# A hybrid decoder trunk with top-2 experts: token lists of all experts from one set of products, expert loops of two engines written out, one projection part moved

## The reference, cut to what matters

```python
D_MODEL, SEQ, N_EXPERTS, TOP_K, D_FF_EXPERT = 1024, 256, 8, 2, 1792

def swiglu(h, w_gu, w_down, d_ff):
    gu = h @ w_gu
    return (jax.nn.silu(gu[..., :d_ff]) * gu[..., d_ff:]) @ w_down

def moe_ffn(h, w_router, w_gu, w_down):
    B, S, D = h.shape
    ht = h.reshape(B * S, D)
    logits = (ht @ w_router).astype(jnp.float32)
    top_vals, top_idx = lax.top_k(logits, TOP_K)
    top_w = jax.nn.softmax(top_vals, axis=-1)
    combine = jnp.sum(jax.nn.one_hot(top_idx, N_EXPERTS, dtype=jnp.float32) * top_w[..., None], axis=1)
    out = jnp.zeros((B * S, D), jnp.float32)
    for e in range(N_EXPERTS):
        y = swiglu(ht, w_gu[e], w_down[e], D_FF_EXPERT)
        out = out + combine[:, e:e + 1] * y.astype(jnp.float32)
    return out.astype(h.dtype).reshape(B, S, D)

# per layer
x = x + token_mixing(rms_norm(x, norm_mix_g[i]), ...)
x = x + swiglu(...) if i % 2 == 0 else x + moe_ffn(rms_norm(x, norm_ffn_g[i]), ...)
h = rms_norm(x, norm_ple_g[i])
x = x + sigmoid(h @ ple_w_gate[i]) * (p[i] @ ple_w_proj[i])
```

## Time and profile before

| | |
|---|---|
| median of 3 runs | 1281.6 us |
| the profiled execution | 1283.54 us |
| its span (first to last instruction) | 1281.8 us |
| TensorE busy | 1216.9 us, 95% |
| VectorE busy | 905.9 us, 71% |
| ScalarE busy | 741.2 us, 58% |
| GpSimd busy | 115.2 us, 9% |
| mean granted TensorE clock | 0.986 |
| chain that ended last, TensorE's share | 78% |

### The profile page before, as it was taken

The page is one execution under the profiler, slowest core; times in us unless marked ns, Lnnn a source line. Parts: engine busy times, 40 slices in busy tenths (PEclk is TensorE's granted clock), DMA queues, the critical chain, the costliest instruction groups (busy, mean ns, idle before and its releaser), DMA issues.

```text
span 1281.8 us, 16174 instructions
## 1 busy us (share of the span) xinstructions
PE 1216.9 (95%) x5978; PEld 1011.5 (79%) x5978; DVE 905.9 (71%) x892; ACT 741.2 (58%) x700; POOL 115.2 (9%) x130
## 2 busy tenths in 40 slices
PE   5999999999999998999999699999999999999977
PEld 4997788788888876997788587777777878787855
DVE  5667756645545566667855678888898888888975
ACT  4536543543543455437443477777777777777753
POOL 3520000200000010420000100000000000001210
PEclk9999999999999999999999899999999999999988
DMA  9845455655555554645454579999999999999941
GB/s 306 289 147 189 140 180 182 191 179 190 196 191 175 191 180 148 195 158 173 135 180 162 179 281 361 373 363 372 367 371 369 370 370 371 358 382 369 391 164 49
DMA packets 167153, 318.47 MB, mean 248 GB/s; under 512 B 6640, under 2 KB 70384, under 8 KB 167104
## 3 DMA queue, kind: packets, MB, share of 16 engines
q1 hardware_dynamic: 161792, 302.01, 67.8%
q0 software_dynamic: 4192, 13.95, 3.0%
q10 hardware_dynamic: 1120, 1.85, 0.4%
HBM read 312.03 MB, written 5.77 MB: 248 GB/s over the span
## 4 chain that ended last, share of the span: by engine, by line
PE 78%; DVE 8%; ACT 7%; issue 4%; DMA 1%; POOL 1%; ACTq 0%; DVEq 0%; SPq 0%; POOLq 0%
PE ps L1591 19%; PE ps L1578 11%; PE ps L1505 10%; PE ps L1357 9%; PE ps L1359 9%; PE ps L1358 9%; PE ps L1519 6%; ACT split L593 5%; DVE split L875 4%; PE ps L1373 1%; DMA raw<-w_in_dram 1%; PE ps L1559 1%; PE ps L1427 1%; DVE M L1162 1%; ACT L593 1%
## 5 line engine op out<-in xcount | busy, mean ns | idle before, releaser
L875 DVE TENSOR_TENSOR split<-raw,split 128x2048 fp32r<-128x2048 f32 x286 | 655.0, 2294 | 258.7 <-ACT split L593 257.8
L593 ACT ACTIVATE split<-raw 128x2048 fp32r<-128x2048 f32 x286 | 546.3, 1915 | 242.3 <-PE ps L1359 103.8
L1591 PE MATMUL ps<-split,br 128*128 128x512 f32 x1344 | 322.7, 395 | 6.9 <-DVE split L875 5.3
L1591 PEld LDWEIGHTS ps<-split,br 128*128 128x128 f32 x1344 | 250.8, 189 | 62.5 <-DVE split L875 9.0
L1357 PE MATMUL ps<-split,hT 128*128 128x512 f32 (+1 forms) x416 | 166.0, 399 | 9.6 <-DVE split L875 4.0
L1578 PE MATMUL ps<-split,hT 128*128 128x512 f32 x672 | 159.1, 392 | 8.7 <-DVE hT L1045 8.7
L1358 PE MATMUL ps<-split,hT 128*128 128x512 f32 (+1 forms) x416 | 161.2, 388 | 0.0
L1359 PE MATMUL ps<-split,hT 128*128 128x512 f32 (+1 forms) x416 | 161.2, 388 | 0.0
L1578 PEld LDWEIGHTS ps<-split,hT 128*128 128x128 f32 x672 | 124.9, 188 | 37.2 <-DVE split L875 11.8
L1505 PE MATMUL ps<-split,hT 128*128 128x512 f32 x576 | 136.5, 392 | 0.5 <-DVE tmp L991 0.5
L1505 PEld LDWEIGHTS ps<-split,hT 128*128 128x128 f32 x576 | 107.1, 188 | 23.3 <-DVE tmp L991 1.2
(11 more groups left out here) (225 smaller groups left out, 1037.6 us busy)
## 6 DMA issues: line engine op xcount, KB each, us to landing
raw<-moe_w_gu_dram SPq DMA_DIRECT2D x96, 1024.0 KB
raw<-moe_w_down_dram SPq DMA_DIRECT2D x56, 1024.0 KB
raw<-w_in_dram SPq DMA_DIRECT2D x46, 1024.0 KB
raw<-ffn_w_gu_dram SPq DMA_DIRECT2D x56, 512.0 KB
raw<-moe_w_gu_dram SPq DMA_DIRECT2D x32, 512.0 KB
raw<-ffn_w_down_dram SPq DMA_DIRECT2D x14, 1024.0 KB
raw<-w_branch_dram SPq DMA_DIRECT2D x12, 1024.0 KB
raw<-w_out_dram SPq DMA_DIRECT2D x8, 1024.0 KB
```

The costliest lines, as they stand in the source:

```text
L593: act.activation(split[:, t % SPLIT, 0, :], raw[:, t % RAW, :], ACT.Copy).then_inc(hi, 1)
L875: dve.tensor_tensor(split[:, t % SPLIT, 1, :], raw[:, t % RAW, :], split[:, t % SPLIT, 0, :].bitcast(F32), ALU.subtract).then_inc(lo, 1)
L1591: ins = pe.matmul(ps[:, 5 if kind == "up" else 4, :], xe[:, sl, 4 * part + k, :], slot(t, sr, 512)[:, k, :], start=part + k + m == 0, stop ...
```

## The change

1. *Lists.* Each token has two picks (k = 0, 1), each with a place in its expert's list (`place2`, from the product with the triangle, masked by `hot`). `build_lists` makes one one-hot matrix for each of 2 token blocks and 2 picks (into `prT`), `tok_hot` holds the token number under its expert's column, and `lists` sums four products to a 128 x 8 matrix: the lists of all eight experts at once. `route`, `take_slots` and the one-hots inside the loop go; G is built for the last expert only.
2. *Loops.* The first pass of the experts is written out in Python on ScalarE and VectorE (TensorE and SyncE keep their loops; the second pass keeps all).
3. *Order in an expert.* The eviction of the transposed activation (tiles 5, 11, 17) is put ahead of that tile's split, on both engines.
4. *Weights.* The weights, rows and picks go into expert 1, at tiles 6, 9 and 12.
5. *Before the experts.* The two token blocks' logits go to banks of their own and VectorE takes them one after the other. The transposes of block 1 come ahead of `proj_part(0, 1)`, `proj_part(1, 0)` behind the second logits, `proj_part(1, 1)` behind the rank; its eviction goes behind the exponential and a split on ScalarE. The tokens-per-expert count has its own product and signal.

```diff
+AT_WEIGHTS = (6, 9, 12)
...
-            def rows_of(s, i, j):
+            def rows_of(s, i):
-                pool.wait_ge(slots_ready[s], j + i)
-                pool.indirect_dma_start(rows_in, None, y_rows[:, :], bass.IndirectOffsetOnAxis(slot_tok[:, 0:1], 0)
+                pool.indirect_dma_start(rows_in, None, y_rows[:, :],
+                                        bass.IndirectOffsetOnAxis(slot_tok[:, i:i + 1], 0)
...
@@ ScalarE, expert @@
+                    if j in AT_EVICT:
+                        act.wait_ge(a_turned[s], AT_EVICT.index(j) + 1 + i * (LAST_F + 1))
+                        act.activation(aT_moe[:, 0], ps[:, 6, :].rearrange("p (k n) -> p k n", k=4), ACT.Copy
+                                       ).then_inc(aT_hi[s], 1)
                     if not last or j + 2 < BODY_TILES:
                         split_hi(t0 + j + 2, i, BODY_TILES, s)
...
-                    if j in AT_EVICT:
-                        act.wait_ge(a_turned[s], AT_EVICT.index(j) + 1 + i * (LAST_F + 1))
-                        act.activation(aT_moe[:, 0], ps[:, 6, :].rearrange("p (k n) -> p k n", k=4), ACT.Copy
-                                       ).then_inc(aT_hi[s], 1)
...
@@ ScalarE, experts @@
-                with act.Fori(0, EXPERTS - 1) as e:
-                    expert(s, t0, e, False)
+                if s == 1:
+                    for e in range(EXPERTS - 1):
+                        expert(s, t0, e, False)
+                else:
+                    with act.Fori(0, EXPERTS - 1) as e:
+                        expert(s, t0, e, False)
...
                     proj_out_of(1, 0)
-                    proj_out_of(1, 1)
-                    act.wait_ge(sel_ready, 2)
+                    act.wait_ge(sel_ready, 3)
                     act.activation(wts[:, :, 1:2], wts[:, :, 0:1], ACT.Exp).then_inc(route_step, 1)
                     split_hi(t0 + T_OUT + 6)
+                    proj_out_of(1, 1)
                     experts(1, t0 + T_FFN[1])
...
@@ VectorE @@
+            def build_lists(s):
+                for b in range(NB):
+                    for k in range(2):
+                        ins = dve.tensor_scalar(prT[:, 2 * b + k, :], slot_row[:, :], place2[:, s - 1, b, k:k + 1],
+                                                None, ALU.is_equal)
+                ins.then_inc(lists_ready[s], 1)
+                dve.wait_ge(route_done[s], 1)
+                dve.tensor_copy(slot_tok[:, :], ps[:, 7, SEQ:SEQ + EXPERTS]).then_inc(slots_ready[s], 1)
...
-                    if j == 1 and not (last and s == 2):
-                        dve.wait_ge(route_done[s], 1 + i)
-                        if not last:
-                            build_g(s, i + 1 + (EXPERTS if s == 2 else 0), g_ready[s])
+                    if last and s == 1 and j == 1:
+                        build_g()
...
-                    if j == AT_MUL[0] and not last:
-                        dve.wait_ge(rows_landed[s], 16 + i * 16)
-                        take_slots(s, 2 + i)
+                    if j in AT_EVICT:
+                        dve.wait_ge(aT_hi[s], AT_EVICT.index(j) + 1 + i * (LAST_F + 1))
+                        dve.tensor_tensor(aT_moe[:, 1], ps[:, 6, :].rearrange("p (k n) -> p k n", k=4),
+                                          aT_moe[:, 0].bitcast(F32), ALU.subtract).then_inc(aT_lo[s], 1)
                     if not last or j + 2 < BODY_TILES:
                         split_lo(t0 + j + 2, i, BODY_TILES, s)
...
+                    if s == 1 and i == 1 and j == AT_WEIGHTS[0]:
+                        token_weights()
+                    if s == 1 and i == 1 and j == AT_WEIGHTS[1]:
+                        token_rows()
+                    if s == 1 and i == 1 and j == AT_WEIGHTS[2]:
+                        token_picks()
...
+                    for b in range(NB):
+                        dve.wait_ge(logit_done, b + 1)
+                        both = ps[:, LOGIT_BANKS[b], 0:2 * EXPERTS]
+                        chain(dve.tensor_copy(logit[:, b, :], both[:, EXPERTS:]))
+                        chain(dve.tensor_tensor(logit[:, b, :], both[:, 0:EXPERTS], logit[:, b, :], ALU.add))
+                        chain(dve.max(top[:, b, :], logit[:, b, :]))
+                        chain(dve.max_index(topi[:, b, :], top[:, b, :], logit[:, b, :]))
+                        chain(dve.tensor_copy(topf[:, b, :], topi[:, b, :]))
+                        chain(dve.tensor_tensor(
+                            hot[:, b], slot_row[:, 0:EXPERTS].unsqueeze(1).broadcast_to([P, 2, EXPERTS]),
+                            topf[:, b, 0:2].unsqueeze(2).broadcast_to([P, 2, EXPERTS]), ALU.is_equal))
+                        dve.tensor_tensor(sel[:, b, :], hot[:, b, 0, :], hot[:, b, 1, :], ALU.add
+                                          ).then_inc(sel_ready, 1)
...
@@ TensorE @@
-            def route(s, n):
-                pe.wait_ge(g_ready[s], n)
-                pe.wait_ge(tok_ready, NB)
+            def lists(s):
+                pe.wait_ge(lists_ready[s], 1)
                 for b in range(NB):
-                    ins = pe.matmul(ps[:, 7, SEQ:SEQ + 1], G[:, b, :].bitcast(F32), tok_f[:, b:b + 1],
-                                    start=b == 0, stop=b == NB - 1)
+                    for k in range(2):
+                        ins = pe.matmul(ps[:, 7, SEQ:SEQ + EXPERTS], prT[:, 2 * b + k, :], tok_hot[:, b, k, :],
+                                        start=b + k == 0, stop=b + k == NB)
                 ins.then_inc(route_done[s], 1)
...
-                    if j == AT_ROUTE and not last:
-                        route(s, 2 + i)
...
                     logits(0)
+                    turn(6, Y, y_of(4), (2, 3))
                     proj_part(0, 1)
-                    turn(6, Y, y_of(4), (2, 3))
+                    logits(1)
                     proj_part(1, 0)
-                    logits(1)
-                    proj_part(1, 1)
...
-                    pe.matmul(ps[:, 6, 80:88], ones[:, :], sel[:, 0, :], start=True, stop=False)
-                    pe.matmul(ps[:, 6, 80:88], ones[:, :], sel[:, 1, :], start=False, stop=True
+                    pe.matmul(ps[:, 6, 72:80], ones[:, :], sel[:, 0, :], start=False, stop=True
                               ).then_inc(rank_done, 1)
+                    pe.matmul(ps[:, 4, 64:72], ones[:, :], sel[:, 0, :], start=True, stop=False)
+                    pe.matmul(ps[:, 4, 64:72], ones[:, :], sel[:, 1, :], start=False, stop=True
+                              ).then_inc(load_done, 1)
+                    proj_part(1, 1)
+                    lists(1)
```

More of the change, by code:

```diff
@@ L185, in trunk @@
         sel = sb("sel", [P, NB, EXPERTS])
[L186 removed]
+        rank = sb("rank", [P, NB])
         load = sb("load", [P, EXPERTS])
@@ L1067, in experts @@
                     gather_lo(s, half, 0)
-                with dve.Fori(0, EXPERTS - 1) as e:
-                    expert(s, t0, e, False)
+                if s == 1:
+                    for e in range(EXPERTS - 1):
+                        expert(s, t0, e, False)
+                else:
+                    with dve.Fori(0, EXPERTS - 1) as e:
+                        expert(s, t0, e, False)
                 expert(s, t0, EXPERTS - 1, True)
@@ L1272, in _ @@
-                    chain(dve.tensor_scalar(rank[:, :, EXPERTS:2 * EXPERTS], rank[:, :, 0:EXPERTS],
-                                            -float(P), None, ALU.add))
-                    take_slots(1, 1)
-                    chain(dve.tensor_copy(load[:, :], ps[:, 6, 80:88]))
-                    chain(dve.tensor_reduce(most[:, 0:1], load[:, :], AX.X, ALU.max))
+                    earlier = ps[:, 6, 64:80].rearrange("p (b e) -> p b e", b=NB)
+                    for b in range(NB):
+                        ins = dve.tensor_tensor(nth[:, b], hot[:, b],
+                                                earlier[:, b].unsqueeze(1).broadcast_to([P, 2, EXPERTS]), ALU.mult)
@@ L1277, in _ @@
+                    chain(dve.tensor_reduce(most[:, 0:1], ps[:, 4, 64:72], AX.X, ALU.max))
                     chain(dve.tensor_scalar(most[:, 1:2], most[:, 0:1], float(P), None, ALU.is_gt))
@@ L1293, in _ @@
-                    place, first, second, row = (pick[:, i] for i in range(4))
-                    for b in range(NB):
-                        for k in range(2):
-                            ins = dve.tensor_tensor(nth[:, b, k, :], hot[:, b, k, :], rank[:, b, 0:EXPERTS],
-                                                    ALU.mult)
-                    chain(ins)
-                    chain(dve.tensor_reduce(place, nth[:, :, :, :], AX.X, ALU.add))
-                    chain(dve.scalar_tensor_tensor(out=row, in0=topf[:, :, 0:2], scalar=float(P), in1=place,
-                                                   op0=ALU.mult, op1=ALU.add))
@@ L1302, in _ @@
-                    chain(dve.tensor_scalar(second, place, float(P), None, ALU.is_ge))
-                    chain(dve.tensor_scalar(first, second, -1.0, 1.0, ALU.mult, ALU.add))
```

(11 more changed lines are left out.)

119 lines of the change are left out of this document (59 added, 60 removed).

## The result

| | before | after |
|---|---|---|
| runs of the comparison | 7 | 7 |
| median (lowest to highest), us | 1281.78 (1280.89 to 1283.37) | 1265.92 (1265.53 to 1273.95) |
| ratio, 95% interval | | 0.990 [0.9881, 0.9919] |
| profiled execution, us | 1283.5 | 1265.92 |
| span, us; mean granted clock | 1281.8; 0.986 | 1264.2; 0.987 |

The median fell by 15.9 us, 16.1 were forecast. The runs of after come in two groups that have to be kept apart: four at 1265.5 to 1265.9 us, clock 0.986 to 0.987, and three at 1273.5 to 1274.0, clock 0.980; the profiled one belongs to the first. The median lies in the lower group by one run. The ratio takes in both groups: the means are 1269.1 and 1282.0 us, 12.8 us apart.

A forecast was written before the change was run, and what follows sets the result against it. TensorE was taken to bound the kernel, but for holes repeating with every expert. The terms 5.8 + 7.8 + 2.0 - 3.2 + 3.5 - 0.6 + 0.8 = 16.1 us gave 1281.6 - 16.1 = 1265.5 us, range 1261.5 to 1274.

The forecast's parts named there:

- Item 1: ScalarE's loop written out: the table load before an expert's tile 2 goes, 6 x 0.97 = 5.8 us; bounds 0 to 5.8.
- Item 2: Eviction ahead of the split: the hole before tile 18 shrinks, 7.8 us, and 2.0 us more in the last expert.
- Item 3: A new 0.45 us wait before tile 20, on the half-size subtraction, 7 times: -3.2 us; bounds 0 to 4.
- Item 4: No list product or one-hot in the loop: 0.50 x 7 = 3.5 us of TensorE; lower bound 2.5.
- Item 5: Weights and picks at tiles 6, 9 and 12 of expert 1 delay VectorE: -0.6 us; bounds 0 and -4.0.
- Item 6: The start, before the experts: 0.8 us sooner; bounds 1.8 sooner, 1.5 later.
- Its 9.4 us: The most gain the forecast's own terms could lose, used for the slow side of the range.
- the start late: Unfavourable bound for the stretch before the experts: 1.5 us later instead of 0.8 sooner.
- DMA rival: Across the experts, transfers become the limit: 1274 us at 375 GB/s, 1279 at 369; chance 0.10.
- starved ring: Evictions three times an expert delay splits TensorE needs; slower if each comes 1.0 us later than worked out; chance 0.04.

The follow-up runs named there:

- e2_loops: Kernel before, with only the loops of ScalarE and VectorE over experts 0 to 6 written out: 1275.80 us, ratio 0.9949.
- e3_loop_dve: Kernel before, with only VectorE's expert loop written out: 1282.67 us, ratio 1.0002.
- e6_tail: Kernel after, with the half-size eviction and subtraction ahead of the second half of the next expert's gathered rows: 1263.51 us, ratio 0.9864.
- e4_lists: Kernel after, with loops, eviction order and place of weights and picks as before; new lists and order before the experts stay: 1285.10 us, ratio 1.0012.
- e8_all: e7_busy with the order of e6_tail and a Silu of one value right behind the exponential: 1261.92 us, ratio 0.9847.
- e9_full: e10_hole with the order of e6_tail, the early one-value Silu and 20 unread matmuls behind the lists: 1257.93 us, ratio 0.9819.
- e7_busy: e5_part_back with 20 matmuls whose result nothing reads, issued behind the lists for the row gather's wait: 1266.71 us, ratio 0.9880.
- e5_part_back: Kernel after, with projection part (0,1) back ahead of block 1's transposes and (1,0) ahead of the second logits: 1266.43 us, ratio 0.9886.
- e10_hole: Kernel after, with 9 matmuls whose result nothing reads ahead of block 1's transposes: 1265.41 us, ratio 0.9881.
- e1_order: Kernel before, with only the evictions of the transposed activation moved ahead of the split on both engines: 1275.10 us, ratio 0.9941.

## Why the prediction was right, item by item

*Item 1, the table load, 5.8 us.* Right in cause and size. e2_loops gives 5.7 us, e3_loop_dve nothing.

*Item 2, eviction ahead of the split, 7.8 + 2.0 us.* Right. The hole before tile 18 shrank by 1.10 us, as worked out, and the last expert by 2.28.

*Item 3, the wait before tile 20, -3.2 us.* Place, cause and length are right (seven times, 0.42 us, on the half-size subtraction). Its price is not: by starts an expert loses 0.69 us there, not 0.45, since a wait of 0.42 also costs TensorE the overlap of one tile with the next (a tile ahead of a wait lasts 2.99 us; in a run of tiles one starts every 2.72). e6_tail gets 0.60 an expert back. That makes 4.8 us, over the item's bound of 4. The 0.24 us an expert that this is more than forecast don't show in the sum, since they came back elsewhere: 0.13 at the start of the expert, whose tiles 0 to 4 with the first transposes take 13.96 us against 15.56 before, where 1.47 were counted, and the rest in amounts too small to place.

*Item 4, the list product, 3.5 us.* 0.5 us an expert (e4_lists: 62.02 against 62.53), but not in expert 0. There it turned into a wait: with the product gone TensorE reached the first transposes before VectorE had the gated product, which stood behind the Silu table load that the written-out code keeps.
```profile
744.04 1.28 ACT L688 ACT_TABLE_LOAD   x1
```
```profile
733.63 16.54 PE L1612 MATMUL ps<-split,br 128*128 128x512 f32 x60 [0.56 <-DVE br L995]
750.72 0.66 PE L1580 MATMUL ps<-ident,tmp 128*128 128x128 f32 x4 [0.55 <-DVE tmp L1040]
```
Expert 0 was to gain 1.1 + 0.5 - 0.45 = 1.15 us and gained 0.08. Its second part, behind the first transposes, gained 0.49 (46.87 against 47.36); its first part lost 0.41 (17.09 against 16.68), of which the wait is a part; some 0.3 more go to the clock, which stays at half for 5.6 us of expert 0 (733.63 to about 739.2) where it did for 4.9 before (735.93 to about 740.8). The forecast used expert 2 for all seven; half clock and the first load make expert 0 another case. With the early Silu in e8_all and e9_full that wait is gone. No run has the early Silu alone, but the other parts leave the wait as it is: it is 0.55 us in e6_tail, which has the order, and 0.55 in e7_busy, where the clock is full.

*Item 5, weights and picks in expert 1, -0.6 us.* Right in size, not in place: expert 1 is 61.20 us, 0.77 over its neighbours. The prediction lets the first two groups of instructions fit and the third pile up. By starts, 0.52 us go behind the first group, which VectorE begins at 818.82 (TensorE's tiles from 819.84 to 828.52 take 8.68 us, 8.16 in expert 2), and 0.28 behind the third, begun at 836.15 (837.17 to 845.61, 8.44 against 8.16). The instructions moved were 24 before, not 23; nothing hangs on it.

*Item 6, the start, 0.8 us sooner.* The working was right and its frame too small. From the second logits' product to the first expert it is 14.59 us (719.04 to 733.63) against 15.45 before (720.48 to 735.93): 0.86 sooner. But the second logits came 1.20 later behind the first, so the start is 0.34 later. The failed step is that the item followed only the part (1,1). The others move too; the one that goes from ahead of the transposes to behind them leaves TensorE idle 2.89 us instead of 1.40, and the clock falls. The prediction reads the clock in two stretches of an expert, where it is full, and says nothing of it here, though it is at half in before as well, from 727.5 to 740.5 us.

*Sum.* 15.3 us were forecast for the experts and 14.2 came; the 1.1 missing are expert 0's. For the start 0.8 was forecast and -0.3 came. So the rows give 13.9 us, and the medians 15.9. The match to 0.4 us is partly luck: what fills the gap lies in the untouched code ahead of and behind the stage, where the granted clock varies from run to run. Which run gets which level there wasn't settled. And one more run of seven in the upper group would have put the median near 1273.5.

*The range.* 1261.5 to 1274 holds the median and, just, the upper group of runs, which came for a reason that the prediction doesn't name. Its 9.4 us can't be found in the three terms that it names: item 5 at its worst (3.4 more), item 4 low (1.0) and the start late (2.3) give 6.7, which is 1272.2 us; the start came later than forecast, within its bound. The upper group is the long half clock at the start. For e4_lists its profile shows that. For after, where no run of the upper group was profiled, it is inferred: the same drop in mean clock (0.987 to 0.980) and the same idle time ahead. The counts bear it out. With the hole of 2.9 us open, 12 of 24 runs lie in an upper group, at a mean clock of 0.979 to 0.981 (three of seven of after, eight of twelve of e4_lists, one of five of e6_tail). With it filled or moved (e5_part_back, e7_busy, e8_all, e9_full, e10_hole) it is none of 22, the lowest clock being 0.983 in one run of e5_part_back, and none of 21 with the order of before (e1_order to e3_loop_dve). That the hole is what opens the way to the upper group is shown by this; what decides it from run to run is not.

*Rivals.* The DMA rival is refuted: 387 GB/s over 24 us and 383 over 350 us, no split behind a landing. The Trainium skill holds two statements on this. "DMA: Bandwidth & Descriptors" (Where 436 GB/s comes from) lets the HBM side bind at about 358 GB/s; the trace is 8% over it. "Perfetto Trace Analysis" (Roofline) says that a core can pull more than that share when it is the only one of its pair that is active; this kernel runs on one core, and the trace agrees with this one. The starved ring is refuted too: TensorE waits for splits 0.4 us in all, twice.

## What to carry to other kernels

Price a hole by the starts of the instructions around it, not by its idle time alone, and treat the first pass of a loop as a case of its own. Where an engine that sets the time gets idle in a short serial stretch, look at its clock behind the gap: here the move of six matmuls cost 1.2 us in the profile of after and some 8 us in three of seven runs. Matmuls of no use in the gaps, with one table load and the half-size eviction and subtraction moved, took 8 us off its median; that eviction and subtraction alone give 2.4 of it (e6_tail). With one gap left (e5_part_back, e7_busy, e10_hole) the upper group was gone, but nothing was won over the better runs of after.

## What the runs showed of the hardware

- ScalarE's loop, with Silu and copies in its body, has two table loads in every pass, at its top and ahead of its first Silu (14 in seven passes); the same code written out has one load for all eight experts. One load is 1.28 us, and the next ACTIVATE starts 1.29 us behind its start (925.98, 927.27). The Trainium skill ("ScalarE: Activation LUTs", What ACT_TABLE_LOAD costs) counts some 1.38 us of drain on top; here the load follows the ACTIVATE before it at once and no such time shows.
- TensorE fell from 2.4 to 1.2 GHz at idle times of 2.89 us (after) and 1.56 us (e5_part_back), and didn't at 1.40 (before), 1.39 (e5_part_back) and 0.71 us (e10_hole), each followed by steady work. The longest idle time alone doesn't tell: in before the clock fell at about 727.2, while the list product ran and ahead of the 5.12 us wait, behind idle times of only 0.75 and 1.04 us with short products between them (it reads 1.00 up to 727, 0.66 from 727.0 to 727.5 and 0.50 from there). Nor did it fall at one place for the same gap: in e7_busy within the 1.56 us, in e5_part_back 1.7 us behind them. How long it stayed differed too: some 4 us in the profile of after, some 30, with the row gather in them, in that of e4_lists.
- Being busy didn't bring it back at once: from 720 to 730 us of e4_lists TensorE is busy all the time by the profile, and the clock reads 0.50. In e7_busy it came back while the 20 matmuls ran, where in e5_part_back, without them, it came back at about 738 (e7_busy: 0.50 from 725 to 730 us, 0.66 from 730 to 735, 1.00 from 735 on).
- The hardware loop of VectorE costs nothing that can be measured here: 1.0002 [0.9994, 1.0011].
